# Hybrid encoder step: the second half's chain in layer 1 placed anew, step by step, on every engine

## What is computed

```python
for layer in range(DEPTH):
    x = rms_norm(h, g[0])
    m = ab_mixer(x) if layer % 2 == 0 else pool_mixer(x, hist)
    h = h + rms_norm(m, g[1])
    h = h + rms_norm(swiglu(rms_norm(h, g[2]), ffn_w_in, ffn_w_out), g[3])

def pool_mixer(xn, hist):               # 4 groups of 256 channels, windows 2, 4, 8, 16
    ext = concatenate([hist, xn])       # hist: the last 15 normalised inputs
    d = window_sum(ext, w) / count - xn
    y = einsum(d, c_w) * c_scale
    return y, ext[-15:]                 # the state rows that are returned

def swiglu(h, w_in, w_out):
    gu = h @ w_in                       # 1024 x 5632
    return (silu(gu[:DFF]) * gu[DFF:]) @ w_out      # DFF = 2816 = 22 blocks of 128
```

## Time and profile before

| | us |
|---|---|
| Median of 3 runs | 1005.46 |
| The profiled execution | 1005.22 |
| its span, first to last instruction | 1003.4 |
| TensorE busy (95%) | 951.0 |
| VectorE busy (74%) | 744.9 |
| ScalarE busy (55%) | 555.9 |
| GpSimd busy (5%) | 52.4 |
| TensorE's granted clock, mean | 0.978 |

### The profile page before, as it was taken

One profiled execution on the slowest core, in us unless ns is written; L12 is line 12 of the kernel. 1 busy time (PEld: TensorE's weight loads), 2 busy tenths in 40 slices (PEclk: granted clock), 3 DMA queues, 4 the chain that ended last, 5 costly groups with the idle time before them and its releaser, 6 DMA issues.

```text
span 1003.4 us, 17818 instructions
## 1 busy us (share of the span) xinstructions
PE 951.0 (95%) x7034; PEld 915.5 (91%) x7034; DVE 744.9 (74%) x1122; ACT 555.9 (55%) x1049; POOL 52.4 (5%) x59
## 2 busy tenths in 40 slices
PE   7999999899999999999999898856999999999997
PEld 5799899899999999999999897746999999999886
DVE  5496555788799998876688766687999988755643
ACT  5633665666555555466566654644555555555542
POOL 0080210100000000000000003000000000000000
PEclk9999999999999999999999998787999999999999
DMA  8323122556444454276555654332444453555643
GB/s 275 86 74 95 43 81 68 148 174 187 139 132 137 127 143 141 70 221 184 171 171 158 181 164 123 103 85 57 142 129 137 130 145 105 159 172 184 210 168 111
DMA packets 246163, 138.66 MB, mean 138 GB/s; under 512 B 15226, under 2 KB 237282, under 8 KB 246080
## 3 DMA queue, kind: packets, MB, share of 16 engines
q1 hardware_dynamic: 245088, 136.54, 47.0%
q10 hardware_dynamic: 768, 0.63, 0.2%
q0 software_dynamic: 224, 0.35, 0.1%
HBM read 134.91 MB, written 2.58 MB: 137 GB/s over the span
## 4 chain that ended last, share of the span: by engine, by line
PE 83%; DVE 7%; issue 4%; ACT 3%; DMA 2%; POOL 1%; ACTq 0%; DVEq 0%; POOLq 0%
PE ps L796 13%; PE ps L798 12%; PE ps L797 12%; PE ps L1253 12%; PE ps L1255 11%; PE ps L1254 11%; PE ps L1205 3%; PE ps L1207 2%; PE ps L1206 2%; DMA raw<-in_ffn_w_in_dram 2%; DVE wlo L1978 2%; ACT whi L1410 1%; PE ps L1172 1%; DMA scale_rows<-in_c_scale_dram 1%; PE ps L1046 1%
## 5 line engine op out<-in xcount | busy, mean ns | idle before, releaser
L1978 DVE TENSOR_TENSOR wlo<-raw,whi 128x1024 fp32r<-128x1024 f32 (+3 forms) x232 | 230.7, 997 | 93.9 <-ACT whi L1410 93.4
L1410 ACT ACTIVATE whi<-raw 128x1024 fp32r<-128x1024 f32 (+3 forms) x232 | 199.4, 864 | 74.7 <-PE ps L798 56.3
L1253 PE MATMUL ps<-xhi,whi 128*128 128x288 f32 (+1 forms) x528 | 154.0, 292 | 1.0 <-ACT tmp L1878 1.0
L1255 PE MATMUL ps<-xhi,wlo 128*128 128x288 f32 (+1 forms) x528 | 153.7, 291 | 0.0
L1254 PE MATMUL ps<-xlo,whi 128*128 128x288 f32 (+1 forms) x528 | 153.3, 290 | 0.0
L797 PE MATMUL ps<-mlo,whi 128*128 128x288 f32 (+1 forms) x528 | 152.7, 289 | 0.0
L1978 DVE TENSOR_TENSOR wlo<-t,whi 128x1024 fp32r<-128x1024 f32 x86 | 105.1, 1223 | 32.5 <-ACT whi L1410 32.5
L1253 PE MATMUL ps<-shi,whi 128*128 128x288 f32 x352 | 105.3, 299 | 16.0 <-DVE slo L2440 15.0
L1205 PE MATMUL ps<-xhi,whi 128*128 128x256 f32 x352 | 105.0, 298 | 13.4 <-ACT p L1835 12.0
L796 PE MATMUL ps<-mhi,whi 128*128 128x288 f32 (+1 forms) x368 | 107.9, 293 | 0.0
L798 PE MATMUL ps<-mhi,wlo 128*128 128x288 f32 (+1 forms) x368 | 107.5, 292 | 0.0
(11 more groups left out here) (304 smaller groups left out, 2127.8 us busy)
## 6 DMA issues: line engine op xcount, KB each, us to landing
raw<-in_ffn_w_in_dram SPq DMA_DIRECT2D x176, 256.0 KB, 3.4
raw<-in_ffn_w_in_dram SPq DMA_DIRECT2D x44, 512.0 KB, 4.1
raw<-in_ffn_w_out_dram SPq DMA_DIRECT2D x48, 384.0 KB, 3.7
raw<-in_ffn_w_out_dram SPq DMA_DIRECT2D x48, 320.0 KB, 3.5
raw<-in_ffn_w_out_dram SPq DMA_DIRECT2D x22, 512.0 KB, 4.0
raw<-in_ab_w_in_dram SPq DMA_DIRECT2D x10, 512.0 KB, 4.4
raw<-in_ab_w_out_dram SPq DMA_DIRECT2D x10, 256.0 KB, 2.9
raw<-in_ab_w_out_dram SPq DMA_DIRECT2D x20, 128.0 KB, 3.3
```

Source lines behind the costliest of these rows:

```text
L1253: pe.matmul(out, wh, hi[:, k, :], start=opens and k == 0, stop=False, skip_group_check=True)
L1255: mm = pe.matmul(out, wl, hi[:, k, :], start=False, stop=k == KC // 2 - 1, skip_group_check=True)
L1410: act.activation(whi[:, m % NSPLIT, 0:n], split_source(m), ACT.Copy).then_inc(w_hi, 1)
L1978: dve.tensor_tensor(wlo[:, s, 0:n], split_source(m), whi[:, s, 0:n].bitcast(F32), ALU.subtract)\
```

## The change

Layer 1's stage no longer uses the common table. A new table `CHAIN` gives each step its own slot on TensorE, ScalarE and VectorE (two lines of it are shown), and a chain function `late_chain` on each engine issues them. In `fast_first` of layer 1 TensorE and ScalarE get a second point in each unit where steps are issued. The x of both norms is made in two parts: h times gain on ScalarE (`weigh`) as soon as h is there, the factor of the norm in one VectorE instruction for a pair of blocks. The first T sums move from unit 19 to slot 3; their weights are loaded after unit 5 of the pass, a second copy of one block (`v2`) in the place of `u2`. The state rows are turned from x (`xf`), so that the guard, the power and GpSimd's product for them go. Both tiles of `c_w` have places of their own and are loaded on SyncE's queue, so the first pass has four raw tiles. The table load of Silu moves behind `r_post`. Stages before and behind this one keep their order.

```diff
-    (1, 1): {"sum": 1, "spread": 3, "scale": (3, 4, 5, 6), "fold": 7, "pre": 7, "again": 9, "x": (9, 9, 10, 11),
-             "hist": 4, "rows": (8, 9), "keep": (9, 10), "c": (11, 12),
-             "windows": (12, 13, 14), "ends": (13, 14), "post": (13, 14, 14, 15), "add": (14, 15, 15, 16)},
...
+CHAIN = {
+    "PE": {"sum": 1, "spread": 1, "hist": 3.5, "pre": 4, "again": 4.5, "c": (5, 5, 5.5, 5.5), "rows": (6, 6), "sum2": 10.5,
...
+    "DVE": {"sum": 0, "scale": (0, 0, 1, 1), "fold": 2, "pre": 3, "terms": (3, 3, 3), "x": (3, 3, 3, 4),
...
         kind, layer, f = unit[0], *(unit[1:3] if unit[0] in ("ta", "tb") else (0, 0))
         if kind == "ta":
+            if (layer, f) == (1, 0):
+                seq.append(("u2", 1, 0))
+                continue
...
+        if unit == ("p", 1, EARLY_TERMS):
+            seq += [(half, 1, 0) for half in ("g1", "u1", "v2", "g2")]
...
-                    sp.dma_start(gain_row[:, :], norm_g[1, 0].partition_broadcast(LAST_ROWS)).then_inc(hist_loaded, 16)
-                if LOADS[r] == ("p", 1, 5):
-                    sp.dma_start(c_tile[:, :].rearrange("p (k n) -> p k n", k=4), c_rows(0)).then_inc(w_loaded[NRAW - 1], 16)
+                    for j, tile in enumerate((c_tile, c_tile_1)):
+                        sp.dma_start(tile[:, :].rearrange("p (k n) -> p k n", k=4), c_rows(j)).then_inc(hist_loaded, 16)
...
             def turn_rows(i):
 
-                pe.wait_ge(h_added[1], 8)
-                if i:
-                    pe.wait_ge(hist_hi, 1)
+                pe.wait_ge(x_scaled[1], 8)
+                pe.wait_ge(wide_kept[1], KC)
                 for q in range(4):
-                    mm = pe.transpose(flat(5 - i, q * P, P, LAST_ROWS), h[:, 4 * i + q, TOK - LAST_ROWS:TOK], ident[:, :])
+                    mm = pe.transpose(flat(5 - i, q * P, P, LAST_ROWS), xf[:, 4 * i + q, TOK - LAST_ROWS:TOK], ident[:, :])
                 mm.then_inc(rows_turned, 1)
...
+            def plain_pool_products(g):
 
                 n = TOK - CUT + HIST + 1
-                tile = raw_tile(NRAW - 1) if j else c_tile
-                if j == 0:
-                    pe.wait_ge(w_loaded[NRAW - 1], c_loaded())
+                tile = c_tile_1 if g >= 2 else c_tile
+                if g == 0:
                     pe.wait_ge(hist_hi, 1)
-                    pe.wait_ge(rows_kept, 2)
                     pe.wait_ge(r_kept[0], KEPT[2, 1])
-                for e in range(4 * j, 4 * j + 4):
-                    g, o = divmod(e, 2)
+                pe.wait_ge(x_scaled[1], 4 + g + 1)
+                for e in range(2 * g, 2 * g + 2):
                     ring = POOL_RING[1]
                     if e >= len(ring):
                         pe.wait_ge(wide_kept[1], e - len(ring) + 1)
-                    pe.wait_ge(x_scaled[1], 4 + g + 1)
                     for k in range(2):
...
+            def late_chain():
+
+                at = CHAIN["PE"]
+                yield at["sum"]
+                sum_squares(1, 1, 0)
+                yield at["spread"]
+                spread(1, 1, 0)
+                yield at["hist"]
+                turn_hist()
+                yield at["pre"]
+                sum_squares(1, 1, 1)
...
                         half_product(f, range(KC // 4, KC // 2), False, True).then_inc(p1_done, 1)
                     else:
                         half_product(f, range(KC // 2), True, True).then_inc(p1_done, 1)
+                        if layer:
+                            run(f)
                         if f != 2:
                             second(f - 1)
                         if f == 1:
                             second(1)
-                    run(f)
+                    run(f + LATER)
...
-                act.wait_ge(rstd_done[1], stat_count(1, 1))
-                act.activation(last_rows[:, 512 * i:512 * (i + 1)], flat(5 - i, 0, 512, LAST_ROWS), ACT.Copy,
-                               scale=rs[0:LAST_ROWS, 6:7]).then_inc(rows_kept, 1)
+                act.activation(last_rows[:, 512 * i:512 * (i + 1)], flat(5 - i, 0, 512, LAST_ROWS), ACT.Copy).then_inc(rows_kept, 1)
...
+            def weigh(s, p):
+
+                act.wait_ge(h_added[1], 4 * s + p + 1)
+                x = xb[1][:, 2 * p:2 * p + 2, :] if s == 2 else xf[:, 2 * p:2 * p + 2, frames(1)]
+                for k in range(2):
+                    op = act.activation(x[:, k, :], h[:, 2 * p + k, frames(1)], ACT.Copy, scale=gain(*X_GAIN[s], 2 * p + k))
+                op.then_inc(weighed, 1)
+
+            def late_chain():
+
+                at = CHAIN["ACT"]
+                yield at["keep"]
+                keep_spread(1, 1, 0)
+                for p, slot in enumerate(at["squares"]):
+                    yield slot
+                    square_pair(1, 1, p)
...
@@ -1831,17 +1896,20 @@
                 for f, m in enumerate(P_PASS[layer]):
                     act.wait_ge(p1_done, n0 + f + 1)
                     if layer and f == 18:
-                        act.wait_ge(rows_scaled, 1)
+                        act.wait_ge(out_stored, 16 * STORES_POOL)
                     act.activation(p1[:, f, 0:CUT], flat(f % 4, 0, CUT), ACT.Copy).then_inc(p1_kept, 1)
                     if f == 0 and layer == 0:
                         evacuate_out(13)
                         hi_part(m + 2)
                         hi_part(m + 3)
                     run(f)
-                    if layer and f == 19:
-                        act.wait_ge(out_stored, 16 * STORES_POOL)
+                    if f == 0 and layer:
+                        warm(ACT.Silu)
                     if f:
+                        if layer and f == 21:
+                            act.wait_ge(w_lo, split_no(AT["ta", 1, 0]))
                         gelu_gate(f - 1)
+                        run(f + LATER / 2)
                         if f < FC - 3 or f == FC - 3 and layer == 0:
                             hi_part(m + 3)
...
             def x_scale(s, b, p):
 
+                if s and b:
+                    x = xb[1][:, 2 * p:2 * p + 2, :] if s == 2 else x_pair(s, b, p)
+                    dve.wait_ge(weighed, 4 * (s - 1) + p + 1)
+                    dve.tensor_tensor(x, x, pair_of(r_pre, 1), ALU.mult).then_inc(x_scaled[b], 1)
...
+            def late_chain():
+
...
+                def norm(s, again):
+                    yield at["sum" + again]
+                    guard(s, 1, 0)
+                    for p, slot in enumerate(at["scale" + again]):
+                        yield slot
+                        if p == 0:
+                            dve.wait_ge(r_kept[1], KEPT[s, 0])
+                        residual_pair(s, 1, p)
+                    yield at["fold" + again]
+                    add_square(s, 1, 3)
+                    fold_squares(s, 1)
+                    yield at["pre" + again]
+                    guard(s, 1, 1)
+
+                yield from norm(1, "")
+                for slot, step in zip(at["terms"], (first_terms, second_term, last_term)):
+                    yield slot
+                    step(1, 0)
+                for p, slot in enumerate(at["x"]):
+                    yield slot
+                    if p == 0:
+                        dve.wait_ge(r_kept[1], KEPT[1, 1])
+                    x_scale(1, 1, p)
+                steps = [*zip(at["windows"], (0, 1, 4, 5, 7, 9), (late_windows,) * 6, range(6)),
+                         *zip(at["mix"], (2, 3, 13, 14), (late_mix,) * 4, range(4))]
+                steps += [(slot, (6, 6, 8, 10, 15, 16, 17, 18)[e], add_mixed, e) for e, slot in enumerate(at["add"])]
+                for slot, _, step, n in sorted(steps, key=lambda step: step[1]):
...
@@ -2514,11 +2635,8 @@
                     elif f == FC - 3:
                         if layer == 0:
                             run(LAST)
-                        first_terms(layer, 0)
-                        second_term(layer, 0)
-                        if layer:
-                            last_term(layer, 0)
-                        else:
+                            first_terms(layer, 0)
+                            second_term(layer, 0)
                             lo_part(AT["ta", layer, 0])
                     elif f == FC - 2:
...
 
             power(3, 1)
-            power(4, 1, True)
-            pool.wait_ge(hist_loaded, 48)
+            power(4, 1)
             pool.wait_ge(rows_kept, 2)
-            pool.tensor_tensor(last_rows[:, :], last_rows[:, :], gain_row[:, :], ALU.mult).then_inc(rows_scaled, 1)
-            pool.wait_ge(rows_scaled, 1)
             pool.dma_start(cp_p[0, 0], last_rows[DEC - HIST:DEC, :]).then_inc(out_stored, 16)
             pool.dma_start(cp_s[0, 0], last_rows[LAST_ROWS - HIST:LAST_ROWS, :]).then_inc(out_stored, 16)
+            pool.wait_ge(out_stored, 16 * STORES_POOL)
             pool.memset(xa[1][:, 0:KC // 2, CUT:TOK - CUT], 0.0)
```

251 lines of the change are left out of this document (148 added, 103 removed).

## The result

The changed kernel takes 970.39 us (four runs, 969.97 to 970.70) against 1005.74 in the runs beside it: a ratio of 0.965 (95% interval 0.9633 to 0.9667), 35.3 us less. The forecast was 974.3 with a gain of 31.2. The profiled execution took 969.97 us, its span is 968.2.

The account below looks back on a forecast made before the run. The second pass's start, set by VectorE's chain of legs, bounds the kernel. Legs plus 1.7 us of hand-offs move it from 685.85 to 656.5 (29.35 us); with 1.9 for the clock, gain 31.2, so 974.3 us; range 968 to 987.

Parts of the forecast that it names:

- What bounds the kernel: Layer 1's stage: the second pass's start, set by the chain of legs on VectorE, reaches the end one for one.
- the clock term: Second pass's first 18 products, at 1.2 GHz after the long wait before: without that wait 1.9 us more gain.
- Gain from slots closed up: x for the pooling to second residual: gain of 15.3 us is slots closed up, more than work removed.
- Leg 1: VectorE's chain up to the first residual: guard 572.8, power 573.7, spread and copy 1.2, residual at 574.9 instead of 583.68.
- Leg 2: First residual to x for the pooling: 15.4 us instead of 24.25, with the power ending after all three T sums.
- Leg 3, 4, 5: x to second residual 30.4 us (before 45.75), to the layer's x 16.3 (17.70), to the second pass 17.8 (14.47).
- Hand-offs: Semaphore latency where two engines meet at new points in the chain: 17 places at 0.1 us, 1.7 us.
- Rival A: TensorE's floor bounds: hand-offs free, chain ahead of TensorE, 77 us work plus 8.4 waits, start 652.1, 969.5 to 970; chance 0.15.
- Rival B: ScalarE and VectorE become the bound in the stage, `whi` waits come back: 983.3, up to 985 us; chance 0.22.
- C: Transfers: `c_w` and the T weights hold up units 4 to 6: start 660, 978 us; chance 0.05.
- D: Slower: many small waits keep TensorE's clock down, 1.13 us a half product, 1013.8 us at 35 of them; chance 0.03.
- Hidden edits: Side edits: GpSimd's state-row work and four tiles nothing; table load 0 to +1.3 us; `c_w` up to +3; T loads up to +2.

## Why the prediction was right, and where it was off

The time lies in the range, 3.9 us under the forecast, and the mechanism held. Three terms of the sum were off by 1 us or more (legs 1 and 2 and the hand-offs), all on the slow side.

- *What bounds the kernel.* Right. The second pass's start moved by 33.25 us and the end by 35.2; the 1.95 behind it are the clock term, forecast as 1.9.
- *Gain from slots closed up.* Right, and shown for the chain: the new slots with the old operations (and the three edits named there) take nearly 30 us, and the leg through the pooling stays at 43.8 without the slots. 16 of the 33 lie in the leg through the pooling, as forecast (15.3).
- *Leg 1.* 1.0 us early: guard at 571.37, not 572.8; from there to the residual 2.5, not 2.1.
- *Leg 2* is the step that was wrong in its mechanism, by 1.3 us. The prediction took the row at 603.08 for how a power fares among VectorE's instructions, and let it wait for three T sums. It got in after the first, as the Trainium skill's "SBUF — State Buffer", section "🔬 SBUF: two separate sides", says of the port pair: whichever of the two starts first holds it for its whole instruction. This case's rows agree: 1.77 us at 585.10, and with one more power ahead 1.48. The one that does not, 2.60 at 603.08, is not explained. One long row had been weighed above the rule; the 1.76 at 578.77 behind a single split fitted either.
- *Leg 3, 4, 5.* Within 0.5 us each.
- *Hand-offs, 1.7 us.* Not there. The four legs of the walk make 79.9 us without them, the chain measured 78.7, and the 1.2 between are the power of leg 2. That durations read from start to start held the latency already is the likely reason; no run tests it. With the legs' differences (-1.0, -1.3, -0.4, +0.1, +0.5) this is the whole 3.9 us between 656.5 and 652.6.
- *Rival A.* Its number (652.1) is nearer than the forecast's, its parts were not: TensorE works 80.7 and not 77 and waits 5.4 and not 8.4. By the time alone the run fits A better than the forecast. What A had right is that hand-offs cost nothing beyond the walk; what it had wrong is a chain ahead of TensorE, which still waits 0.89 us for `slo`. Nor is TensorE's list as it stands the floor: with its longest wait filled the chain is as long, though the lead did not last.
- *Rival B* fell: VectorE was 88% busy, as forecast, with 0.1 us of waits for `whi`. Those 11.9 us were an effect of the order, not of full lists. Small signs of B are the copies for which TensorE waits (0.47 us at 650.02).
- *C* fell: with three tiles too, ScalarE waited for no weights at units 4 to 6.
- *D* fell for the stage (mean clock 0.98), but its argument was too kind to short waits: behind 1.91 us the clock was 0.71 in the changed kernel. How far it fell differed from trace to trace and moved the second guard by up to 0.8 us where all else was equal (10.98 and 11.81 behind the first residual). Behind 5.97 us the second pass lost 2.1.
- *Hidden edits.* The four tiles are worth 0.3 us in the new order, hardly more than nothing. The table load's move was put at nothing; in the old order the wait of 3.43 us ahead of the first residual went with it (and with earlier weights), so its share there is open. Moving the gain to ScalarE brings 0.7 to 0.9 us in the chain, hardly to be seen in the time. Of the early T sums the prediction said only that their absence is counted in the last units: they are worth 3.5 us, by ScalarE's list. GpSimd's product for the state rows was costed at nothing, and that was wrong at least in what it held up. GpSimd, then VectorE, in the kernel before:

```profile
614.38 2.77 POOL L2746 TENSOR_TENSOR last_rows<-last_rows,gain_row 64x1024 f32<-64x1024 f32 x1 [7.88 <-ACT last_rows L1717]
```

```profile
610.79 0.94 DVE L2256 SCALAR_TENSOR_TENSOR xf<-h,gains,r_pre 128x288 f32<-128x288 f32 x2
...
614.84 3.05 DVE L2256 SCALAR_TENSOR_TENSOR xf<-h,gains,r_pre 128x288 f32<-128x288 f32 x2
```

The two instructions for x at 614.84 take 3.05 us instead of 0.94: the first, of 2.62 (to 617.46), ended only when GpSimd's product (614.38 to 617.15) was over. That is the odd one in the mean of 0.774. 2.1 us of the old leg of 45.75 may have been this: in the kernel with the old slots, which has no such product, that leg is 1.9 shorter. But other edits are in it too, and the state rows' edit was not tried alone, so its share stays open.

## What to carry to other kernels

Measure such a change by the legs of the chain, start to start on one engine, and say for each what stands queued behind each wait on every engine; here that gave three of four legs within 0.5 us, and the fourth but for one term of contention. When a step is moved, look at what comes to stand behind it on the other engines: T sums late and spread late each lost 3.5 us by a copy that was stuck behind the moved step, not by the step, and with all slots late 4.0 us were the slot itself and some 4.6 what came to stand elsewhere and the clock. Before a difference of one leg is put down to an edit, compare the granted clock of the stretch ahead of it: one late guard here was the clock's doing. Filling a wait only pays when the chain can use it.

## What the hardware showed

In every row but one, a power of GpSimd got in after the one VectorE instruction that ran, also where the next followed at once: it took 1.46 to 1.80 us when it met a split or T sum of 1.22, 0.85 with VectorE idle. The exception is the 2.60 us at 603.08 behind two splits, which stays open. The other way round, GpSimd's product of 64 x 1024 (2.77 us) held a VectorE instruction of 0.51 us for 2.62.

TensorE's clock behind a wait of 1.91 us differed between traces: 0.50, 0.63, 0.69, 0.71, 0.75 and 1.00 as the mean of 5.5 us, with products 0.21 us apart instead of 0.12 where it was down. Behind the wait of 0.89 us for `slo`, and behind several of 0.6 to 1.3 us in the kernel with all slots later, it stayed at 1.00. Behind 5.97 us the loss was 2.1 us.
